# Decoder-layer kernel: key roots of the cached sequences on GpSimd as a power, page numbers read once

## The chip, the cores and the metric

The kernel runs on one core of one Trainium2 chip. The core has a TensorE (PE), which multiplies matrices out of SBUF into PSUM, a VectorE (DVE), a ScalarE (ACT), a GpSimd (POOL) and a SyncE (SP), whose queue here issues nearly all loads. Each engine works through its own instructions in order and waits on semaphores of the others. The metric is device microseconds of one execution.

## The reference, cut to what matters

One layer of a decoder is applied to 512 prompt positions and to 8 cached sequences of 4 new positions each (544 columns in all). The part at issue is the attention of the new positions over a paged latent cache of 2048 rows, 16 pages of 128 rows per sequence:

```python
def decompress(latent, lw):
    kv = (latent @ lw['w_kvb']).reshape(*latent.shape[:-1], H_A, NOPE_DIM + V_DIM)
    return rmsnorm(kv[..., :NOPE_DIM], lw['g_kn']), kv[..., NOPE_DIM:]

def one(args):                       # one cached sequence
    pt, qn, qr, lat_n, kr_n = args
    lat = jnp.concatenate([cache_latent[layer, pt].reshape(past, KV_LORA), lat_n], 0)
    kr = jnp.concatenate([cache_krope[layer, pt].reshape(past, ROPE_DIM), kr_n], 0)
    k_nope, v = decompress(lat, lw)
    s = (jnp.einsum('qhd,khd->hqk', qn, k_nope) + jnp.einsum('qhr,kr->hqk', qr, kr)) * scale
    ...
    p, _ = softmax_stats(s)
    return jnp.einsum('hqk,khd->qhd', p, v)
```

`rmsnorm` of a key of 64 numbers divides it by the root of its mean square plus 1e-6. Every cached key of every one of the 8 heads needs such an inverse root: 2048 rows x 8 heads per sequence.

## The kernel before

**The program as a whole.** Input projections, query projection, norms and rotations come first (to about 341 us), then the attention of the prompt (341 to 493 us), the eight cached sequences (493 to about 801 us), and then the output projection, the feed-forward part and the last gate (to the end). The matmuls of the projections are made of three products of split numbers (`mm3`, L494).

**A cached sequence (b = 0..7).** The keys themselves are not normed. The scores are taken by absorbed queries straight from the transposed latent page (`pgT`), and then multiplied by the inverse root of each key, so the keys are made only for the sum of their squares. For each of 16 pages t:

- ACT rounds the page to its upper half (`page_hi`, L737), DVE makes the lower half (`page_lo`, L1272), three pages ahead;
- PE makes the page's 512 raw key numbers in 6 matmuls (`page_keys`, L999), into one of two halves of `ps[0]`;
- ACT squares them (`page_square`, L744) into one of two halves of `sqK`, and DVE adds them up to 8 columns of `ssq` (`page_sums`, L1278).

PE may begin page g only when page g-2 is squared, and ACT may square page g only when page g-2 is summed.

**Behind the 16 pages.** PE takes the scores (`scores`, L1015, L1019) and the window scores (`win_scores`, L1031). ACT takes the root of the 128 x 128 numbers of `ssq` (`key_root`, L748). DVE, in its `scores` (L1283 and on), waits for that root, takes the reciprocal (L1284), transposes it to the layout of the scores (L1285), multiplies the scores by it (L1289) and finds row maxima, up to `mX` (L1300).

**The tails.** The rest of sequence b is laid between the pages of sequence b+1: PE at page 2 takes `row_max` (L1040, needs `mX`), at page 7 `values` (L1050 needs the exponentials and the window values `cV`; L1056 the latent pages `pgL`), at page 11 `turned` (L1065, L1068). ACT at page 3 takes the exponentials (L753, L754), at page 8 the scaled outputs. DVE at page 2 reads the maxima, at page 4 transposes the exponentials (L1311).

**The loads.** SP issues for each sequence, in this order: wait for the scores of the sequence before; pages 8 to 15 of this sequence (`load_pages`, L552); the window keys `cK` (L559); pages 0 to 7 of the next; wait for the values of the sequence before; 16 latent pages `pgL` (`load_latent`, L556); the window values `cV` (L562, L565). Each load of a page needs its page number, which SP reads from `ptab` into a register (`page_number`, L547): a TENSOR_LOAD and two instructions more. Each page is loaded twice, once as `pgT` and once as `pgL`, so its number is read twice.

**GpSimd.** It multiplies for the rotations (L421), issues the copies of the caches to the outputs (L614, L618) at marks of the other engines' progress, and has nothing to do between 461 and 898 us.

**The new rows.** The same inverse root is taken once for the 32 new rows (`rkN`): sums by DVE (L1194), root by ACT (L709), reciprocal by DVE (L1196), just ahead of the prompt's attention. DVE needs it in `p_new` (L1258) only, but the wait stands ahead of the loop.

Of the kernel before, what the change touches and what calls it, by code (L numbers as in the profile page):

```python
# [29 lines left out]
ACT = mybir.ActivationFunctionType  # L30
ALU = mybir.AluOpType
# [3 lines left out]
P = 128  # L35
D = 1024
KD = D // P
NP_ = 512
NB, NQ = 8, 4
NS = NB * NQ  # L40
T = NP_ + NS
HT = T // 2
H = 8
# [9 lines left out]
POOL = 160  # L53
# [16 lines left out]
RING = 24  # L70
NBUF = 4
AHEAD = 3
S_NEW, S_WIN, S_WNEW, S_ALL = 512, 544, 768, 800


# [30 lines left out]
def build(nc, x, cst, gains, win, wqb, wk, wv, wkt, wo, wgu, wdn, wdn2, wpl, plt, pgt, pgl, ck, cv, pt,  # L106
          y, o_lat, o_kr, o_ks, o_vs, o_ck, o_cv):
    with ExitStack() as ctx:
# [12 lines left out]
        def sb(name, shape, dt=F32):  # L121
            n = 1
            for x in shape[1:]:
                n *= x
            return at(name, shape, room(n), dt)

        def sem(name):
            return ctx.enter_context(nc.semaphore(name))
# [59 lines left out]
        mr, m2, nm, den, rec = (sb(n, [P, 2]) for n in ("rowmax", "rowmax2", "negmax", "den", "recip"))  # L188
        mX = sb("mX", [P, 2, 4])
        warm = sb("warm", [P, 1])  # L190
        st = sb("st", [P, 16])
        ptab = sb("ptab", [1, NB * NPG], I32)

# [26 lines left out]
        p_qg, p_ab, p_all = (sem(n) for n in ("prep_qg", "prep_absorb_mm", "prep_all"))  # L220
        q_ab, p_new, p_nw, z_new, k_raw, k_sq, k_ss, k_rt = (sem(n) for n in (
            "queries_laid", "new_scores_mm", "new_scores", "new_rows_cleared", "kraw_mm", "kraw_sq", "kraw_ssq", "key_root"))
        m_sc, w_sc, m_sub, w_max, m_x, m_mx, m_nm, m_e, m_et = (sem(n) for n in (
            "mla_scores", "win_scores", "mla_scores_read", "win_scores_read", "rowmax_masked", "max_mm", "max_read",
            "exp", "exp_turned"))
# [301 lines left out]
        @block.sync  # L527
        def _(sp):
            sp.dma_start(hT[:, 0:2, :], x[:, 0:2, :]).then_inc(s_x[0], 16)
            sp.dma_start(G[:, :], gains).then_inc(s_g, 16)  # L530
            sp.dma_start(C[:, 0:C_MA], cst[:, 0:C_MA]).then_inc(s_c, 16)
            for k in range(1, KD // 2):
                sp.dma_start(hT[:, 2 * k:2 * k + 2, :], x[:, 2 * k:2 * k + 2, :]).then_inc(s_x[k], 16)
            for u in range(2):
                sp_weight(W_IN + u, win[u])
            sp.dma_start(C[:, C_MA:], cst[:, C_MA:]).then_inc(s_c2, 16)
            sp.dma_start(wK[:, :, :], wk).then_inc(s_wk, 16)
            sp.dma_start(wV[:, :, :], wv).then_inc(s_wk, 16)
            sp.dma_start(ptab[:, :], pt).then_inc(s_pt, 16)
            for u in range(2, NIN):  # L540
                sp_weight(W_IN + u, win[u])
            for u in range(H):
                sp_weight(W_QB + u, wqb[u])
            for u in range(2):
                sp_weight(W_O + u, wo[u])
            def page_number(b, t):
                return bass.ds(sp.value_load(ptab[0:1, b * NPG + t:b * NPG + t + 1], min_val=0, max_val=POOL - 1), 1)  # L547

            def load_pages(b, ts):
                for t in ts:  # L550
                    s = (b * NPG + t) % RING
                    sp.dma_start(pgT[:, s, :], pgt[page_number(b, t), :, :].rearrange("a p n -> p (a n)")).then_inc(pg_in[s], 16)  # L552

            def load_latent(b):
                for t in range(NPG):
                    sp.dma_start(pgL[:, t, :], pgl[page_number(b, t), :, :].rearrange("a p n -> p (a n)")).then_inc(pl_in, 16)  # L556

            def load_win_k(b):
                sp.dma_start(cK, ck[b, :, :, PAST - W_TAIL:PAST].rearrange("c p n -> p c n")).then_inc(ck_in, 16)  # L559

            def load_win_v(b):
                sp.dma_start(cV[:, 3:NTW, :], cv[b, PAST - REC:PAST, :].rearrange("(j p) n -> p j n", p=P)).then_inc(cv_in, 16)  # L562
                for u in range(3):
                    old = cv[b, u * P * 4:(u + 1) * P * 4, :].rearrange("(g r) n -> g r n", r=16)
                    sp.dma_start(cV[:, u, :], old[:, 0:4, :]).then_inc(cv_in, 16)  # L565

            sp.wait_ge(s_pt, 16)
            sp.wait_ge(cq_lo, KQ)
            load_pages(0, range(11))
            sp.wait_ge(a_pv, 4 * H)  # L570
            sp.dma_start(wkT, wkt).then_inc(s_wkt, 16)
            load_win_k(0)
            sp.wait_ge(p_read, 2)
            load_latent(0)
            sp.wait_ge(a_o, H)
            sp.wait_ge(out_s, 80)
            sp.wait_ge(p_nw, 1)
            load_pages(0, range(11, NPG))
            load_pages(1, range(RING - NPG))
            load_win_v(0)  # L580
            for b in range(1, NB):
                sp.wait_ge(m_sc, b)
                load_pages(b, range(RING - NPG, NPG))
                sp.wait_ge(w_sc, b)
                load_win_k(b)
                if b + 1 < NB:
                    load_pages(b + 1, range(RING - NPG))
                sp.wait_ge(m_pv, b)
                load_latent(b)
                sp.wait_ge(w_pv, b)  # L590
                load_win_v(b)
            for u in range(2, KD):
                sp_weight(W_O + u, wo[u])
            sp.wait_ge(w_pv, NB)
            sp.dma_start(plT, plt).then_inc(s_plt, 16)
            sp_weight_loop(W_GU, 2 * HALVES[0], wgu[0:2 * HALVES[0]])
            sp_weight_loop(W_DN, KD, wdn)
            sp_weight_loop(W_GU2, 2 * HALVES[1], wgu[2 * HALVES[0]:])
            sp_weight_loop(W_DN2, KD, wdn2)
            sp_weight_loop(W_PL, KD, wpl)  # L600
            for m in range(KD):
                sp.wait_ge(pl_ev[m % 2], m // 2 + 1)
                sp.dma_start(y[m], hT[:, m, :]).then_inc(out_y, 16)
            sp.wait_ge(out_y, 16 * KD)

        @block.gpsimd
        def _(pool):
# [9 lines left out]
            def copy_v(b, z):  # L617
                pool.dma_start(o_cv[b, z * HALF:(z + 1) * HALF, :],  # L618
                               cv[b, NQ + z * HALF:NQ + (z + 1) * HALF, :]).then_inc(out_c, 16)

            pool.memset(vNew[:, :], 0.0).then_inc(z_new, 1)
            pool.memset(latNew[:, :], 0.0).then_inc(z_new, 1)
            pool.wait_ge(z_new, 2)
# [7 lines left out]
            for g in g_qh:  # L631
# [8 lines left out]
            pool.dma_start(o_cv[:, PAST - NQ:PAST, :].rearrange("b q n -> b (q n)"),  # L640
                           vNew[0:NS, :]).then_inc(out_s, 16)
            pool.wait_ge(out_s, 80)
            for k in range(8):
                pool.wait_ge(a_s, 8 * k + 1)
                copy_v(k // 2, k % 2)

            for b in range(4, NB):
                for k in range(4):
# [5 lines left out]
        def _(act):  # L654
# [50 lines left out]
            act.activation(tmp[0:NS, 0, 0:512], ps[0][0:NS, 0, :], ACT.Square).then_inc(kn_sq, 1)  # L705
            act.wait_ge(tn_mm, 1)
            act.activation(latNew[0:NS, :], ps[0][0:NS, 1, 0:KVL], ACT.Copy).then_inc(tn_ev, 1)
            act.wait_ge(kn_ss, 1)
            act.activation(rkN[:, :], rkN[:, :], ACT.Sqrt, scale=1.0 / NOPE, bias=G[0:NS, G_EPS:G_EPS + 1]).then_inc(k_rt, 1)  # L709


            for n in range(len(units) + 4):
# [30 lines left out]
                    act.wait_ge(k_ss, g - 1)  # L743
                act.activation(sqK[:, g % 2, :], ps[0][:, g % 2, :], ACT.Square).then_inc(k_sq, 1)  # L744

            def key_root(b):
                act.wait_ge(k_ss, (b + 1) * NPG)
                act.activation(ssq[:, b % 2, :], ssq[:, b % 2, :], ACT.Sqrt, scale=1.0 / NOPE,  # L748
                               bias=G[:, G_EPS:G_EPS + 1]).then_inc(k_rt, 1)

            def exps(b):
                act.wait_ge(m_nm, b + 1)
                act.activation(E[:, 0:S_WIN], S[:, 0:S_WIN], ACT.Exp, bias=nm[:, 0:1], accum_out=den[:, 0:1])  # L753
# [12 lines left out]
            for b in range(NB):  # L766
                for t in range(NPG):
                    page_square(b, t)
                    if b * NPG + t + AHEAD < NB * NPG:
                        page_hi(*divmod(b * NPG + t + AHEAD, NPG))  # L770
                    if b and t in act_tail:
                        act_tail[t](b - 1)
                key_root(b)
            for t in act_tail:
                act_tail[t](NB - 1)
            sqrt_table()
# [369 lines left out]
        def _(v):  # L1146
# [46 lines left out]
            v.wait_ge(kn_sq, 1)  # L1193
            v.tensor_reduce(rkN[:, :], tmp[0:NS, 0, 0:512].rearrange("p (h d) -> p h d", h=H), AX.X, ALU.add).then_inc(kn_ss, 1)  # L1194
            v.wait_ge(k_rt, 1)
            link(v.reciprocal(rkN[:, :], rkN[:, :]))  # L1196
            for n in range(len(units) + 5):
                if n >= 2 and n - 2 < len(units):
                    m = n - 2
# [33 lines left out]
                    link(v.memset(qwS, 0.0))  # L1233
                if n == 20:
                    v.wait_ge(n_rope, ropes_before[-1])
                    v.tensor_scalar(qg[:, :, :], QT[LOW, :, NP_:T], G[LOW, G_K:G_K + 1], None, ALU.mult).then_inc(p_read, 1)
                    for j in range(4):
                        last = v.tensor_copy(qrB[32 * j:32 * j + 32, :, 32 * j:32 * j + 32].rearrange("p b (h q) -> p h b q", h=H),
                                             QT[MID, :, NP_:T].rearrange("p h (b q) -> p h b q", q=NQ))
                    last.then_inc(p_read, 1)  # L1240
                    v.wait_ge(p_read, 2)
                    v.sem_inc(q_ab, 1)
# [37 lines left out]

            def scores(b):

                v.wait_ge(k_rt, b + 2)  # L1283
                link(v.reciprocal(ssq[:, b % 2, :], ssq[:, b % 2, :]))  # L1284
                link(v.transpose(RK, ssq[:, b % 2, :].unsqueeze(2).broadcast_to([P, NPG * H, NQ])))  # L1285
                v.wait_ge(m_sc, b + 1)
                if b:
# [277 lines left out]
```

## Time and profile before

| | us |
|---|---|
| median of 3 runs | 1374.35 |
| lowest, highest | 1372.84, 1376.12 |
| the profiled execution | 1373.12 |
| its span, first to last instruction | 1371.3 |
| PE busy in it | 1263.7 |
| DVE busy | 593.0 |
| ACT busy | 485.9 |
| POOL busy | 45.7 |
| mean granted TensorE clock | 0.926 of 2.4 GHz |

All times in the rows are from the start of the span of that one execution. A busy time of PE is modelled from the starts of its matmuls, so PE shows busy also where it paces nothing; who waits for whom tells more. Only the stretch from 493 to 801 us holds the work that is changed, together with a few instructions at 342 us.

### The profile page before, as it was taken

To read this page: it belongs to the slowest core of one execution; us is meant where nothing else is said; L and a number is where in the kernel's file an instruction comes from. 1 tells how busy PE (TensorE), PEld (TensorE's weight loads), DVE (VectorE), ACT (ScalarE), POOL (GpSimd) and SP (SyncE) were. 2 spreads that over 40 slices of the span, in tenths; PEclk is the share of its full clock that TensorE was granted. 3 is DMA by queue.
4 is the path that set the end of the run, shared out by engine and by line. 5 is a ranking of instruction groups with operands and counts; after the bars stand their busy time and mean duration, and the time that the engine had idled before them with its cause. 6 is when DMAs were issued, how large, how long until landed. Compare 5 with 4: busy or idle time off the path is not lost.

```text
span 1371.3 us, 22076 instructions
## 1 busy us (share of the span) xinstructions
PE 1263.7 (92%) x8308; PEld 1034.4 (75%) x8308; DVE 593.0 (43%) x1095; ACT 485.9 (35%) x861; POOL 45.7 (3%) x60
## 2 busy tenths in 40 slices
PE   5999989999999999998889778799999999999798
PEld 4988976434655576665566458699999999999788
DVE  4223221644774456665556435643332223333543
ACT  4223243101653355554455332333332112222332
POOL 0000000321000000000000000000000000000000
PEclk8999999956997589999999968899999999999899
DMA  6773312002445135666566602155464354562122
GB/s 236 251 271 141 116 36 87 0 1 83 184 164 213 61 110 159 224 225 204 181 216 198 223 26 70 66 201 201 165 208 175 138 180 157 199 225 97 57 77 85
DMA packets 68820, 202.70 MB, mean 148 GB/s; under 512 B 7457, under 2 KB 40226, under 8 KB 67394
## 3 DMA queue, kind: packets, MB, share of 16 engines
q1 hardware_dynamic: 66562, 131.74, 28.9%
q0 software_dynamic: 2176, 69.90, 14.1%
q8 instruction: 48, 0.79, 0.2%
q14 instruction: 34, 0.28, 0.1%
HBM read 196.53 MB, written 72.13 MB: 196 GB/s over the span
## 4 chain that ended last, share of the span: by engine, by line
PE 72%; SPq 14%; DVE 6%; issue 5%; ACT 1%; DMA 1%; DVEq 0%; ACTq 0%
PE ps L494 48%; SPq L547 7%; PE ps L947 4%; PE ps L387 4%; PE ps L967 4%; SPq L556 3%; SPq L552 3%; PE ps L398 3%; PE ps L956 2%; PE ps L410 2%; PE ps L999 2%; DVE R L435 1%; DVE tmp L452 1%; DVE aLo L353 1%; PE ps L911 1%
## 5 line engine op out<-in xcount | busy, mean ns | idle before, releaser
L494 PE MATMUL ps<-aHi,wHi 128*128 128x272 f32 (+1 forms) x1392 | 296.7, 295 | 37.2 <-DVE aLo L353 33.8
L494 PE MATMUL ps<-aHi,wLo 128*128 128x272 f32 (+1 forms) x1392 | 292.7, 292 | 0.0
L494 PE MATMUL ps<-aLo,wHi 128*128 128x272 f32 (+1 forms) x1392 | 291.7, 291 | 0.0
L494 PEld LDWEIGHTS ps<-aHi,wHi 128*128 128x128 f32 (+1 forms) x1392 | 220.7, 190 | 47.2 <-issue 19.5
L366 DVE TENSOR_TENSOR wLo<-ring,wHi 128x1024 fp32r<-128x1024 f32 (+3 forms) x105 | 133.4, 1271 | 211.5 <-ACT wHi L361 211.5
L494 PEld LDWEIGHTS ps<-aLo,wHi 128*128 128x128 f32 (+1 forms) x1392 | 222.0, 190 | 0.0
L494 PEld LDWEIGHTS ps<-aHi,wLo 128*128 128x128 f32 (+1 forms) x1392 | 220.6, 191 | 0.0
L361 ACT ACTIVATE wHi<-ring 128x1024 fp32r<-128x1024 f32 (+3 forms) x105 | 114.5, 1091 | 196.3 <-PE ps L494 196.2
L1278 DVE TENSOR_REDUCE ssq<-att 128x8 f32<-128x512 f32 x128 | 87.4, 683 | 97.2 <-ACT att L744 96.1
L744 ACT ACTIVATE att<-ps 128x512 f32<-128x512 f32 x128 | 76.3, 596 | 117.7 <-PE ps L999 117.1
L999 PE MATMUL ps<-wkHi,pgHi 128*128 128x512 f32 x256 | 103.2, 403 | 11.6 <-ACT att L744 10.4
L999 PE MATMUL ps<-wkHi,pgLo 128*128 128x512 f32 x256 | 100.0, 391 | 0.0
L999 PE MATMUL ps<-wkLo,pgHi 128*128 128x512 f32 x256 | 99.7, 390 | 0.0
L494 PE MATMUL ps<-hidHi,wLo 128*128 128x272 f32 x352 | 72.9, 288 | 0.0
L494 PE MATMUL ps<-hidHi,wHi 128*128 128x272 f32 x352 | 72.7, 288 | 0.0
L387 PE MATMUL ps<-sq,C 128*128 128x272 f32 (+5 forms) x196 | 59.7, 458 | 14.2 <-ACT sq L295 14.2
L494 PE MATMUL ps<-hidLo,wHi 128*128 128x272 f32 x352 | 72.6, 288 | 0.0
L999 PEld LDWEIGHTS ps<-wkHi,pgHi 128*128 128x128 f32 x256 | 48.1, 188 | 25.9 <-issue 15.7
L724 ACT ACTIVATE att<-att,st 128x128 f32<-128x128 f32 (+1 forms) x64 | 36.0, 562 | 67.5 <-DVE st L1217 66.6
L1362 DVE TENSOR_TENSOR sq<-ps,tmp 128x544 f32<-128x544 f32 x22 | 16.0, 725 | 101.3 <-ACT tmp L803 101.3
L737 ACT ACTIVATE pgHi<-big 128x256 fp32r<-128x256 f32 x128 | 52.3, 410 | 19.2 <-DMA big<-in_pgt 19.2
L1272 DVE TENSOR_TENSOR pgLo<-big,pgHi 128x256 fp32r<-128x256 f32 x128 | 53.0, 416 | 13.8 <-ACT pgHi L737 13.8
(181 smaller groups left out, 1521.5 us busy)
## 6 DMA issues: line engine op xcount, KB each, us to landing
out_o_cv<-in_cv POOLq DMA_DIRECT2D x16, 2044.0 KB, 8.3
ring<-in_wgu SPq DMA_DIRECT2D x44, 512.0 KB, 3.5
big<-in_pgt SPq DMA_DIRECT2D x128, 144.0 KB, 2.8
big<-in_pgl SPq DMA_DIRECT2D x128, 128.0 KB, 2.0
kv<-in_ck SPq DMA_DIRECT2D x8, 1792.0 KB, 8.5
ring<-in_win SPq DMA_DIRECT2D x21, 512.0 KB, 4.2
kv<-in_cv SPq DMA_DIRECT2D x8, 1024.0 KB, 5.5
kv<-in_cv SPq DMA_DIRECT2D x24, 256.0 KB, 5.7
```

Of the source, the lines that this page charges most:

```text
L361: nc.scalar.activation(wHi[:, u % 2, 0:width], ring[:, u % 2, 0:width], ACT.Copy).then_inc(w_hi, 1)
L366: nc.vector.tensor_tensor(wLo[:, u % 2, 0:width], ring[:, u % 2, 0:width], wHi[:, u % 2, 0:width].bitcast(F32), ALU.subtract).then_inc(w_l ...
L387: last = nc.tensor.matmul(ps[2][out, a, 0:hw], ones, sq[rows, k % 2, a * hw:(a + 1) * hw], start=(j == 0 and t == 0), stop=(j == len(q["sr ...
L494: ins = nc.tensor.matmul(pair[rows, a, 0:HT], w[:, c], xx[:, k, a * HT:(a + 1) * HT], start=(k == 0 and z == 0), stop=(k == nk - 1 and z = ...
L547: return bass.ds(sp.value_load(ptab[0:1, b * NPG + t:b * NPG + t + 1], min_val=0, max_val=POOL - 1), 1)
L737: act.activation(pgHi[:, g % NBUF, :], pgT[:, g % RING, 0:KVL], ACT.Copy).then_inc(p_hi, 1)
L744: act.activation(sqK[:, g % 2, :], ps[0][:, g % 2, :], ACT.Square).then_inc(k_sq, 1)
L947: mm(ps[0][:, n % 2, 0:(i + 1) * P], q[:, i * P:(i + 1) * P], k[:, 0:(i + 1) * P], start=True, stop=True).then_inc(a_s, 1)
L967: last = mm(ps[2][r, (h // 2) % 2, i * P:(i + 1) * P], v[:, j, (h % H) * HD:(h % H + 1) * HD], prT[:, m % 2, j * P:(j + 1) * P], start=(j ...
L999: last = mm(ps[0][:, g % 2, :], x_[:, g % NBUF, c * P:(c + 1) * P], w_[:, c, :], start=(c == 0 and z == 0), stop=(c == KC - 1 and z == 2))
L1272: v.tensor_tensor(pgLo[:, g % NBUF, :], pgT[:, g % RING, 0:KVL], pgHi[:, g % NBUF, :].bitcast(F32), ALU.subtract).then_inc(p_lo, 1)
L1278: v.tensor_reduce(ssq[:, b % 2, t * H:(t + 1) * H], sqK[:, g % 2, :].rearrange("p (h d) -> p h d", h=H), AX.X, ALU.add).then_inc(k_ss, 1)
```

## The change

- The page number is kept in a register from its first reading for `pgT` until its reading for `pgL`, and not read again. The eleven numbers of sequence 0 that are read first, and every later pair, follow this; five of sequence 0 are read twice, since their latent pages are asked for first.
- ACT's `key_root` is gone and with it DVE's reciprocal of `ssq`. GpSimd adds 64 x 1e-6 to the sums and raises them to the power -1/2, first for the 12 pages that are summed first (128 x 96 numbers), then for the other 4 (128 x 32). DVE waits for the second one.
- The same for `rkN` (32 x 8), ahead of GpSimd's eight copies of the window values, behind its wait for the outputs of the states.
- The power is taken of the sum, not of the mean, so the absorbed queries are multiplied by 8 (the root of 64), in an instruction that was there.

```diff
+EARLY = 12
+        minus_half = sb("minus_half", [P, 1])
+        z_half, k_eps = sem("half_set"), sem("ssq_eps")
-            def page_number(b, t):
-                return bass.ds(sp.value_load(ptab[0:1, b * NPG + t:b * NPG + t + 1], min_val=0, max_val=POOL - 1), 1)
+            numbers = {}
+
+            def page_number(b, t, last=False):
+                if (b, t) not in numbers:
+                    numbers[b, t] = sp.value_load(ptab[0:1, b * NPG + t:b * NPG + t + 1], min_val=0, max_val=POOL - 1)
+                return bass.ds(numbers.pop((b, t)) if last else numbers[b, t], 1)
...
-                    sp.dma_start(pgL[:, t, :], pgl[page_number(b, t), :, :].rearrange("a p n -> p (a n)")).then_inc(pl_in, 16)
+                    sp.dma_start(pgL[:, t, :], pgl[page_number(b, t, True), :, :].rearrange("a p n -> p (a n)")).then_inc(pl_in, 16)
...
+            pool.memset(minus_half[:, :], -0.5).then_inc(z_half, 1)
...
             pool.wait_ge(out_s, 80)
+            def inverse_root(sums, rows, cols, n):
+
+                pool.tensor_scalar(sums, sums, NOPE * EPS, None, ALU.add).then_inc(k_eps, 1)
+                pool.wait_ge(k_eps, n)
+                pool.tensor_tensor(sums, sums, minus_half[rows, 0:1].broadcast_to([rows.stop, cols]), ALU.pow).then_inc(k_rt, 1)
+
+            pool.wait_ge(z_half, 1)
+            pool.wait_ge(kn_ss, 1)
+            inverse_root(rkN[:, :], slice(0, NS), H, 1)
             for k in range(8):
                 pool.wait_ge(a_s, 8 * k + 1)
                 copy_v(k // 2, k % 2)
+
+            for b in range(NB):
+                pool.wait_ge(k_ss, b * NPG + EARLY)
+                inverse_root(ssq[:, b % 2, 0:EARLY * H], FULL, EARLY * H, 2 * b + 2)
+                pool.wait_ge(k_ss, (b + 1) * NPG)
+                inverse_root(ssq[:, b % 2, EARLY * H:], FULL, P - EARLY * H, 2 * b + 3)
...
-            act.wait_ge(kn_ss, 1)
-            act.activation(rkN[:, :], rkN[:, :], ACT.Sqrt, scale=1.0 / NOPE, bias=G[0:NS, G_EPS:G_EPS + 1]).then_inc(k_rt, 1)
...
-            def key_root(b):
-                act.wait_ge(k_ss, (b + 1) * NPG)
-                act.activation(ssq[:, b % 2, :], ssq[:, b % 2, :], ACT.Sqrt, scale=1.0 / NOPE,
-                               bias=G[:, G_EPS:G_EPS + 1]).then_inc(k_rt, 1)
...
-                key_root(b)
...
             v.wait_ge(k_rt, 1)
-            link(v.reciprocal(rkN[:, :], rkN[:, :]))
...
-                    v.tensor_scalar(qg[:, :, :], QT[LOW, :, NP_:T], G[LOW, G_K:G_K + 1], None, ALU.mult).then_inc(p_read, 1)
+                    v.tensor_scalar(qg[:, :, :], QT[LOW, :, NP_:T], G[LOW, G_K:G_K + 1], NOPE ** 0.5, ALU.mult,
+                                    ALU.mult).then_inc(p_read, 1)
...
-                v.wait_ge(k_rt, b + 2)
-                link(v.reciprocal(ssq[:, b % 2, :], ssq[:, b % 2, :]))
+                v.wait_ge(k_rt, 2 * b + 3)
                 link(v.transpose(RK, ssq[:, b % 2, :].unsqueeze(2).broadcast_to([P, NPG * H, NQ])))
```

**SP, from the last page load `pgT` to the first latent pages `pgL`.** Before:

```order
L552 ISA
L552 DMA big<-in_pgt 128x288
L547 TENSOR_LOAD ptab
L547 ISA x2
L556 ISA
L556 DMA big<-in_pgl 128x256
```

In the change (the same place; L553 is the reading of a number, L559 `pgT`, L563 `pgL`):

```order
L553 TENSOR_LOAD ptab
L553 ISA x2
L559 ISA
L559 DMA big<-in_pgt 128x288
L563 ISA
L563 DMA big<-in_pgl 128x256
L563 ISA
L563 DMA big<-in_pgl 128x256
```

The three instructions that read the number are gone ahead of each latent page; those ahead of the `pgT` pages stay.

**ACT, from the last pages of a sequence to the exponentials of its tail.** Before (L748 is the root, L753 and L754 the exponentials, L744 a square, L737 a page's upper half):

```order
L737 ACTIVATE pgHi<-big 128x256
L748 ACT_TABLE_LOAD
L748 ACTIVATE ssq<-ssq,G 128x128
L744 ACTIVATE att<-ps 128x512
...
L753 ACT_TABLE_LOAD
L753 ACTIVATE C,den<-C,negmax 128x544
L754 ACTIVATE C,den<-C,negmax 128x256
L744 ACTIVATE att<-ps 128x512
```

In the change (L765 is a square, L758 an upper half, L769 and L770 the exponentials):

```order
L765 ACTIVATE att<-ps 128x512
L758 ACTIVATE pgHi<-big 128x256
L769 ACTIVATE C,den<-C,negmax 128x544
L770 ACTIVATE C,den<-C,negmax 128x256
L765 ACTIVATE att<-ps 128x512
```

The root is gone from ACT's order, and so are both table loads, here and at every sequence.

**GpSimd, in the stretch of the cached sequences, where it had nothing before.** In the change, two sequences:

```order
L653 TENSOR_SCALAR ssq<-ssq 128x96
L655 TENSOR_TENSOR ssq<-ssq,minus_half 128x96
L653 TENSOR_SCALAR ssq<-ssq 128x32
L655 TENSOR_TENSOR ssq<-ssq,minus_half 128x32
L653 TENSOR_SCALAR ssq<-ssq 128x96
```

The additions and powers stand between the eight copies of window values and the copies of the feed-forward stretch.

## Rows read from the trace of the kernel before

**Rows 1.** Waits of PE, 519 to 800 us: us in total, times, longest.

```profile
PE ps L1050 <- DMA kv<-in_cv: 19.3, 5, 5.2
PE ps L999 <- ACT att L744: 10.4, 7, 1.5
PE ps L1040 <- DVE mX L1300: 1.9, 1, 1.9
```

**Rows 2.** Waits of SP's queue, whole span: the longest of the stage.

```profile
SPq L547 <- PE ps L1019: 8.7, 1, 8.7
```

**Rows 3.** Windows from scores to scores: us, busy PE, PEld, DVE, ACT, POOL, clock, DMA.

```profile
550.30:585.00 34.70, 32.95 (x231) 23.79 (x230) 21.25 (x49) 19.36 (x41) 0.00 (x0) 1.00 0.67 222
...
619.80:660.60 40.80, 35.88 (x235) 24.75 (x235) 21.49 (x50) 19.36 (x41) 0.00 (x0) 0.92 0.63 204
660.60:699.40 38.80, 34.62 (x235) 24.20 (x238) 21.51 (x50) 19.35 (x41) 0.00 (x0) 0.96 0.66 211
699.40:737.30 37.90, 32.94 (x235) 24.08 (x235) 21.47 (x50) 19.36 (x41) 0.00 (x0) 1.00 0.66 210
737.30:777.90 40.60, 34.60 (x235) 24.18 (x235) 21.15 (x48) 18.75 (x39) 0.00 (x0) 0.96 0.61 199
```

**Rows 4.** Timeline of SP's issues: start, us, what; one round's pages and latent pages, and five rounds later.

```profile
557.87 7.96 SPq L552 DMA_DIRECT2D big<-in_pgt  x8
...
576.12 16.69 SPq L556 DMA_DIRECT2D big<-in_pgl  x16
...
752.84 8.53 SPq L552 DMA_DIRECT2D big<-in_pgt  x8
```

**Rows 5.** SP's instructions for a page number and a latent page: ns min/median/max.

```profile
L547 SPq TENSOR_LOAD <-ptab x256: 262/268/472, 217.5 to 780.6; - x128
L547 SPq FUSED_REGOPS  x256: 152/152/187, 218.0 to 781.2; - x128
...
L556 SPq DMA_DIRECT2D big<-in_pgl x128: 328/333/3114, 407.0 to 781.6; - x128
```

**Rows 6.** Timeline of ACT about the exponentials of one tail.

```profile
596.56 1.28 ACT L753 ACT_TABLE_LOAD   x1
...
599.09 0.57 ACT L744 ACTIVATE att<-ps 128x512 f32<-128x512 f32 x1
```

**Rows 7.** Timeline of DVE from a sequence's last sums to its `mX`; row_max on PEld.

```profile
584.42 0.69 DVE L1278 TENSOR_REDUCE ssq<-att 128x8 f32<-128x512 f32 x1 [0.34 <-ACT att L744]
...
585.78 0.69 DVE L1278 TENSOR_REDUCE ssq<-att 128x8 f32<-128x512 f32 x1 [0.34 <-ACT att L744]
...
587.80 0.95 DVE L1284 RECIPROCAL ssq<-ssq 128x128 f32<-128x128 f32 x1 [1.00 <-ACT ssq L748]
588.78 0.71 DVE L1285 STREAM_TRANSPOSE C<-ssq 128x512 f32<-128x512 f32 x1
...
591.66 0.17 DVE L1300 TENSOR_TENSOR mX<-C,rowmax 128x8 f32<-128x8 f32 x1
...
592.25 0.42 PEld L1040 LDWEIGHTS ps<-mX,C 128*128 128x128 f32 x2
```

**Rows 8.** Timeline of the tail of the last sequence, PE and DVE.

```profile
786.39 1.01 DVE L1311 STREAM_TRANSPOSE big<-C 128x800 f32<-128x800 f32 x1 [1.40 <-ACT C L754]
...
790.00 2.78 PE L1050 MATMUL ps<-kv,big 128*32 128x512 f32 x11 [5.21 <-DMA kv<-in_cv]
```

**Rows 9.** Timeline of POOL: its first, a usual and its longest multiplication.

```profile
144.04 2.33 POOL L421 TENSOR_TENSOR tmp<-big,C 32x544 f32<-32x544 f32 x1 [8.54 <-DVE big L459]
238.66 1.34 POOL L421 TENSOR_TENSOR tmp<-big,C 128x544 f32<-128x544 f32 x1 [92.28 <-DVE big L459]
...
271.88 3.37 POOL L421 TENSOR_TENSOR tmp<-big,C 128x544 f32<-128x544 f32 x1 [2.75 <-DVE big L476]
```

**Rows 10.** Timeline at the new rows' root, DVE and ACT.

```profile
342.61 0.19 DVE L1196 RECIPROCAL rkN<-rkN 32x8 f32<-32x8 f32 x1 [0.37 <-ACT rkN L709]
...
342.60 1.28 ACT L724 ACT_TABLE_LOAD   x1
```

## The prediction

> **What bounds the kernel now.** I first asked where PE waits while the cached sequences run, since its matmuls fill most of the span. Between 519 and 800 us the waits [rows 1] name two causes that matter: 19.3 us in five waits on the window values `cV`, and 10.4 us in seven waits of at most 1.5 us on ACT's squares. The first is not a slow transfer. SP's own waits [rows 2] show that it stood still for 8.7 us once, at the start of the stage, and nowhere else in it for over 2 us: SP issues all the time, and what it issues last in a round comes late. Its round is (752.84 - 557.87) / 5 = 38.99 us [rows 4]. The windows from scores to scores [rows 3] show the other limit. The second sequence takes 34.7 us at full clock with no wait on a load, as do the first and the third (515.5 to 619.8 us for the three, 34.75 each). There SP still lives on its lead. From the fourth on they take 40.8, 38.8, 37.9 and 40.6 us, and the clock falls in three of them. So the bound is **PE at 34.75 us a sequence while SP is ahead, and SP at 39 when its lead is used up**.
>
> **The page numbers.** A latent page takes SP (16.69 - 0.33) / 15 = 1.09 us, of which the issue itself is 0.333 [rows 4, 5]. The reading of a number is 0.268 + 0.152 us of instructions and the short gaps between them: at least 0.42, at most 1.09 - 0.33 = 0.76 us. I take 0.57, which leaves 0.15 for a check of the number and the gaps. Sixteen times this, 9.1 us, leaves a round: 38.99 - 9.1 = 29.9 us (26.8 to 32.3 by the two bounds). All of these are under PE's 34.75, so SP has to wait again and is no bound by any of the bounds. Behind a reading stand only SP's own loads. With SP ahead, the four late sequences take 34.75 us like the first three: 158.1 - 139.0 = **19.1 us less**. Of this 14.1 us are four of the waits on `cV` [rows 1, 3]; the rest is the halved clock that came with them. What comes late next? The loads have room: latent pages every 0.52 us are 252 GB/s while they last, which is above the 222 GB/s of a round of 34.7 us, but the DMA engines were busy for 0.67 of that round [rows 3], and nobody waits for a latent page within 20 us of its issue.
>
> **The table loads.** Without a root on ACT the order has no table load in the sequences. The one at the root costs nothing on the path: ACT waits for PE behind it. The other stands ahead of the exponentials: 1.28 us, and the square behind it starts at 599.09 [rows 6]. PE waits at most 1.5 us for that square, seven times, 10.4 us together [rows 1]. The two exponentials themselves stay. So 7 x 1.28 = **9.0 us less** (10.4 at most, if the whole wait goes), and a sequence becomes 34.75 - 1.28 = 33.47 us, still above SP's 29.9. The eighth load, at the last tail, was hidden. In the row the exponential follows its load without idle time. The Trainium skill (ScalarE: Activation LUTs, What ACT_TABLE_LOAD costs) gives 1283 ns for the load, as here, and 1380 ns of drain beside it for every switch; with a drain on the path the saving would reach the cap of 10.4 us, and the trace has no room for it.
>
> **The root moved to GpSimd.** From the end of a sequence's last sums (585.78 + 0.69 = 586.47) to the start of the transposition (588.78) pass 2.31 us: the rest of the table load, the root, and a reciprocal of 0.95 us [rows 7]. `mX` is ready at 591.83, and PE loads it at 592.25 without waiting. So the new path may take 2.31 + 0.42 = 2.73 us before PE waits. It holds an addition and a power of 128x32, if the power of 128x96, begun four pages earlier, is done. A page is 585.78 - 584.42 = 1.36 us, four are 5.44. No row shows a power on GpSimd. The nearest are its multiplications [rows 9]: 1.34 us for 544 columns, 2.5 ns a column, and 3.37 us, 6.2 ns a column, at its slowest. By either, both parts are over in under 0.8 us, and DVE goes on about 1.9 us earlier than before, which PE does not feel, since it did not wait. A power is surely more work than a product, so these rows are poor bounds above. What decides is the break-even: the first part is hidden up to 5.44 / 96 = 56 ns a column, the second up to some (2.73 - 0.2) / 32 = 79 ns; together PE waits from about 61 ns, **24 times a multiplication**. I take it below that, and the cost as 0. DVE also loses eight reciprocals, which lie in the same path. What GpSimd has queued behind these waits are its copies of the feed-forward stretch, at 898 us.
>
> **The last tail.** After the last sequence nothing covers these steps. PE waited 1.9 us for `mX` [rows 1]; I let it come 1.0 us earlier (0 at 61 ns a column, 1.9 at the price of the multiplication). The transposed exponentials were ready at 786.39 + 1.01 = 787.40, the matmuls started at 790.00 for want of `cV` [rows 8]: 2.6 us. **3.6 us less.** The clock was at half in much of 785 to 833 us; if it falls less, up to 3 us more are won, which I only put in the range.
>
> **The new rows.** DVE waited 0.37 us for ACT, and took 0.19 for the reciprocal [rows 10]. GpSimd now does two instructions of 8 columns in its place. Its wait for the state outputs stands ahead, but it issued its next copy at 343 us only since PE's first scores came then. The table load for the first exponential, 1.28 us from 342.60, no longer has to follow the root and may come earlier. Between -0.5 and +1.0 us (the first multiplication took 2.33 against 1.34 [rows 9]); I take 0. The rescaled queries cost the same instruction.
>
> **The sum.** 19.1 + 9.0 + 3.6 = 31.7 us. The profiled execution took 1373.12 us, 1.2 below the median of the runs; 1373.1 - 31.7 = 1341.4, and against the median **1342.6**.
>
> **Rivals.**
> First, **the power is slow**. This is the way to a slower kernel. With c ns a column, the path is 0.4 + 128c - 5.44 us once the first part is late, and its excess over 2.73 us falls on PE eight times, since `row_max` stands in PE's order ahead of page 2. At 75 ns it is 1.8 us, 15 in all: 1357. At 91 ns (37 multiplications) the 31.7 us are used up. Beyond that the kernel is slower; at 123 ns (50 multiplications) 8.0 x 8 = 64 us against 31.7: 1406. [...]
> Second, **the change does not do what it says for SP**: the issues take back what the readings gave up. One issue of a latent page took 3.11 us [rows 5], at a time when a copy between caches ran. If the round stays at 39 us, PE stays bound by SP, the table loads are hidden too, and the time is 1370 to 1374. Against it: in the stage sixteen issues took 16.69 us without one that blocked.
> Third, **ACT's wait does not go**, since the two exponentials or DVE's transposition end it anyway: 9 us less gain, 1351.
> Fourth, **the first power is slow once**. The row shows 1.0 us more for GpSimd's first multiplication: 1343.6. The Trainium skill (GPSIMD Engine Reference, 2.1 Instruction dispatch) gives about 6 us for the first call of freshly loaded code; by it, ahead of the prompt's attention and uncovered, the time would be near 1348.
>
> **How the numbers follow.** Forecast 0.64; slow power with part of the gain left 0.10, with none 0.08; SP's round unchanged 0.05; ACT's wait stays 0.06; a slow first power, by several us, 0.07. The range reaches up over the third and fourth rival and to 75 ns a column, and down by the clock and the upper bounds of the savings (1.4 + 0.9 + 0.5 + 3, and a little for a steadier clock in the sequences): 1335 to 1358. A measurement of this kernel can tell about 0.2%, 2.7 us, from no change. Faster by more: 0.64 + 0.10 + 0.06 + 0.07 and half of SP's case, 0.89. Within: 0.03. Slower: 0.08.
>
> **What would show it.** SP waits again for scores or values in every round, some 3 us in each. Scores follow scores every 33.5 us in all eight sequences, at full clock, and no wait on `cV` is left, also in the tail. PE's seven waits on the square shrink to about 0.2 us. GpSimd's power of 128x96 takes under 5.4 us and that of 128x32 under 2.5. PE never waits for `mX` in the sequences. Wrong would be the forecast if PE waits at `row_max`, if the latent pages still come 1.09 us apart, or if a load named in PE's waits has taken SP's place.

## The result

The change makes the kernel slower: 1475.1 us (median of 4 runs, 1471.7 to 1477.3) against 1374.9 before, a ratio of 1.073 (95% interval 1.070 to 1.075). The forecast was 1342.6 us, with a range up to 1358. What came is the first rival, far out: the power on GpSimd costs 160 ns a column, 65 times a multiplication. The two savings in the sum are real, as the experiments below show, and near it in total, though one came out 4 us smaller than forecast and the other 3 us larger: with both of them and the roots left on ScalarE, the kernel takes 1343.8 us.

The changed kernel's page, its first part and one group of the fifth (name, shape, count | busy us, mean ns):

```profile
span 1475.4 us, 21708 instructions
PE 1279.9 (87%) x8308; PEld 1045.9 (71%) x8308; DVE 583.1 (40%) x1086; ACT 461.1 (31%) x836; POOL 223.2 (15%) x95
...
L655 POOL TENSOR_TENSOR ssq<-ssq,minus_half 128x96 f32<-128x96 f32 (+1 forms) x16 | 168.7, 10547 | 1.3
```

POOL is busy for 223.2 us, where it had 45.7. It is busy for 15% of the span and still sets the pace, which only the waits show. Those of PE, 519 to 910 us (us in total, times, longest):

```profile
PE ps L1055 <- DVE mX L1314: 113.2, 8, 16.7
PE ps L1065 <- DVE big L1325: 4.5, 8, 2.7
```

The 19.3 us on `cV` and the 10.4 us on ACT's squares of [rows 1] are gone, both of them. In their place PE waits 113.2 us for `mX`, eight times. And `mX` is late because DVE, which works in order, has to stop ahead of the transposition until GpSimd is done. The timelines of POOL and DVE about the end of the second sequence, which answer to [rows 7]:

```profile
568.34 0.56 POOL L653 TENSOR_SCALAR ssq<-ssq 128x96 f32<-128x96 f32 x1 [26.65 <-DVE ssq L1293]
568.99 15.66 POOL L655 TENSOR_TENSOR ssq<-ssq,minus_half 128x96 f32<-128x96 f32 x1
584.73 0.29 POOL L653 TENSOR_SCALAR ssq<-ssq 128x32 f32<-128x32 f32 x1
585.10 5.43 POOL L655 TENSOR_TENSOR ssq<-ssq,minus_half 128x32 f32<-128x32 f32 x1
...
573.03 0.69 DVE L1293 TENSOR_REDUCE ssq<-att 128x8 f32<-128x512 f32 x1 [0.34 <-ACT att L765]
...
590.57 0.71 DVE L1299 STREAM_TRANSPOSE C<-ssq 128x512 f32<-128x512 f32 x1 [16.52 <-POOL ssq L655]
593.44 0.17 DVE L1314 TENSOR_TENSOR mX<-C,rowmax 128x8 f32<-128x8 f32 x1
```

The last sums end at 573.72. The first part of the power, begun when 12 pages were summed, ends only at 584.65, 10.9 us behind them, and the second runs after that. From the last sums to the transposition pass 16.85 us, where it was 2.31 and could be 2.73.

The windows from scores to scores (columns as in [rows 3]) show the sequences. They alternate between 48.9 and 50.0 us, and the clock is down:

```profile
523.40:572.30 48.90, 34.76 (x233) 24.89 (x232) 20.18 (x49) 16.27 (x38) 22.00 (x5) 0.86 0.50 148
572.30:622.30 50.00, 35.92 (x235) 25.74 (x237) 20.20 (x49) 16.26 (x38) 21.98 (x5) 0.83 0.54 170
622.30:671.20 48.90, 34.80 (x231) 24.92 (x230) 20.10 (x48) 16.27 (x38) 21.88 (x5) 0.86 0.53 167
```

Where the 104.1 us of the span come from, by the starts of the same matmuls in both traces: 7.9 by the first scores (523.4 against 515.5; 3.2 of these are there already when PE begins the prompt's scores, at 345.07 against 341.86, ahead of every changed instruction of this stage, 1.6 are the root of the new rows; beside the rest stands a longer stretch at half clock, 27.3 us from 336.4 on, where it was 17.1 us from 331.4 on), 83.4 in the seven sequences that follow (345.7 against 262.3), 12.5 in the last tail, up to the matmuls that turn the summed latents into outputs (36.1 against 23.6). What comes after is the same within 0.3.

### The profile page after: what moved, and what is told of

Read it like the earlier page. It is cut to its first block, busy times and chain, and to the rows that moved or that the text cites. A ratio compares the mean times of both kernels' runs of the same rounds, so it can differ in the third digit from the quotient of the medians.

```text
span 1475.4 us, 21708 instructions
## 1 busy us (share of the span) xinstructions
PE 1279.9 (87%) x8308; PEld 1045.9 (71%) x8308; DVE 583.1 (40%) x1086; ACT 461.1 (31%) x836; POOL 223.2 (15%) x95
## 4 chain that ended last, share of the span: by engine, by line
PE 75%; POOL 12%; DVE 9%; ACT 2%; issue 1%; DMA 0%; SPq 0%; DVEq 0%; ACTq 0%; POOLq 0%
PE ps L497 45%; POOL ssq L655 11%; PE ps L1014 7%; PE ps L390 4%; PE ps L962 4%; PE ps L982 3%; PE ps L401 2%; PE ps L971 2%; PE ps L413 2%; DVE R L438 1%; PE ps L1071 1%; DVE tmp L455 1%; PE ps L1065 1%; PE ps L926 1%; DVE aLo L356 1%
## 5 line engine op out<-in xcount | busy, mean ns | idle before, releaser
L497 PE MATMUL ps<-aHi,wHi 128*128 128x272 f32 (+1 forms) x1392 | 296.5, 295 | 38.1 <-DVE aLo L356 34.7
L655 POOL TENSOR_TENSOR ssq<-ssq,minus_half 128x96 f32<-128x96 f32 (+1 forms) x16 | 168.7, 10547 | 1.3
L765 ACT ACTIVATE att<-ps 128x512 f32<-128x512 f32 x128 | 76.4, 597 | 242.4 <-PE ps L1014 241.9
L1014 PE MATMUL ps<-wkHi,pgHi 128*128 128x512 f32 x256 | 108.9, 426 | 1.6 <-DVE pgLo L1287 1.2
L1014 PE MATMUL ps<-wkLo,pgHi 128*128 128x512 f32 x256 | 104.7, 409 | 0.0
L1014 PE MATMUL ps<-wkHi,pgLo 128*128 128x512 f32 x256 | 104.5, 408 | 0.0
L1055 PE MATMUL ps<-mX,C 128*128 128x8 f32 x16 | 4.8, 372 | 113.2 <-DVE mX L1314 113.2
L1055 PEld LDWEIGHTS ps<-mX,C 128*128 128x128 f32 x16 | 4.0, 311 | 116.6 <-DVE mX L1314 116.6
L621 POOL DMA_DIRECT2D out_o_ck<-in_ck x16 | 8.1, 507 | 419.4 <-PE ps L497 419.4
L1014 PEld LDWEIGHTS ps<-wkHi,pgHi 128*128 128x128 f32 x256 | 51.9, 203 | 17.1 <-issue 5.6
```

The costliest lines, as they stand in the source:

```text
L497: ins = nc.tensor.matmul(pair[rows, a, 0:HT], w[:, c], xx[:, k, a * HT:(a + 1) * HT], start=(k == 0 and z == 0), stop=(k == nk - 1 and z = ...
L655: pool.tensor_tensor(sums, sums, minus_half[rows, 0:1].broadcast_to([rows.stop, cols]), ALU.pow).then_inc(k_rt, 1)
L1014: last = mm(ps[0][:, g % 2, :], x_[:, g % NBUF, c * P:(c + 1) * P], w_[:, c, :], start=(c == 0 and z == 0), stop=(c == KC - 1 and z == 2))
```

## The experiments

Each is timed beside the kernel before on the same chip: 1374.3 us for the first four, 1376.3 for the last two.

### The page numbers read once, alone

The kernel before with this edit:

```diff
+            numbers = {}
+
+            def page_number(b, t, last=False):
+                if (b, t) not in numbers:
+                    numbers[b, t] = sp.value_load(...)
+                return bass.ds(numbers.pop((b, t)) if last else numbers[b, t], 1)
...
-                    sp.dma_start(pgL[:, t, :], pgl[page_number(b, t), :, :]...
+                    sp.dma_start(pgL[:, t, :], pgl[page_number(b, t, True), :, :]...
```

> The kernel before with the page numbers read once, and nothing else: the roots stay on ScalarE. My theory of the kernel before (SyncE is the bound from the fourth cached sequence on): the four late sequences fall from 158.1 to 139.0 us, and the last tail no longer waits for the window values, 2.6 us. 1374.9 - 21.7 = 1353 us, scores follow scores every 34.75 us, and no wait on the window values is left. Rival (the issues take back what the readings gave up): latent pages still about 1.09 us apart, 1372 to 1375 us.

Measured: 1356.1 us, ratio 0.987 (0.985 to 0.989). The saving is 18 us of the 21.7 expected. All seven sequences take 34.7 us at full clock. Two of the windows, two of SP's issues of 16 latent pages, and two of its waits:

```profile
590.70:625.40 34.70, 32.94 (x231) 23.82 (x230) 21.29 (x50) 19.33 (x41) 0.00 (x0) 1.00 0.74 238
729.60:764.30 34.70, 32.94 (x235) 23.83 (x237) 20.95 (x48) 18.73 (x39) 0.00 (x0) 1.00 0.67 212
...
542.76 8.05 SPq L560 DMA_DIRECT2D big<-in_pgl  x16
...
681.21 9.13 SPq L560 DMA_DIRECT2D big<-in_pgl  x16
...
SPq L550 <- PE ps L1023: 36.8, 7, 8.4
SPq L560 <- PE ps L1060: 8.5, 1, 8.5
```

SP, which waited 8.7 us once [rows 2], now waits for the scores in each of the seven rounds, 36.8 us together. The rival is out: the latent pages are (8.05 - 0.33) / 15 = 0.51 to 0.59 us apart (the prediction had 0.52), where they were 1.09.

### The table of the exponentials loaded early, roots left on ScalarE

```diff
+        def exp_table():
+            nc.scalar.activation(warm[:, :], G[:, G_EPS:G_EPS + 1], ACT.Exp)
...
                 key_root(b)
+                exp_table()
```

> The kernel before with the page numbers read once, and, behind ScalarE's root of each sequence, one exponential of a 128x1 tile that nobody reads, so that the table of the exponentials is loaded there, where ScalarE has 3.5 us to spare, and not ahead of the real exponentials. Roots stay on ScalarE, reciprocals on VectorE. Theory (the saving of the changed kernel's ScalarE part was real and is to be had without GpSimd): seven times 1.28 us less than with the numbers alone, 1353 - 9 = 1344 us, scores follow scores every 33.5 us. Rival (the two exponentials end the wait anyway): the same 1353 us as with the numbers alone.

Measured: 1343.8 us, ratio 0.977 (0.974 to 0.979), 12 us below the numbers alone. Timeline of ACT at the end of the third sequence, and at the exponentials:

```profile
587.13 1.28 ACT L756 ACT_TABLE_LOAD   x1
588.42 0.40 ACT L756 ACTIVATE ssq<-ssq,G 128x128 f32<-128x128 f32 x1
588.84 1.28 ACT L342 ACT_TABLE_LOAD   x1
590.13 0.20 ACT L342 ACTIVATE warm<-G 128x1 f32<-128x1 f32 x1
592.37 0.60 ACT L752 ACTIVATE att<-ps 128x512 f32<-128x512 f32 x1 [2.03 <-PE ps L1008]
...
597.49 0.74 ACT L761 ACTIVATE C<-C,negmax 128x544 f32<-128x544 f32 x1
```

Both loads now lie where ACT would be idle, and 2.0 us are still left there. The exponentials at 597.49 come without one ahead. The windows say what that is worth, and that nothing else took its place:

```profile
519.50:552.80 33.30, 32.96 (x232) 23.80 (x231) 21.30 (x50) 19.45 (x42) 0.00 (x0) 1.00 0.67 205
552.80:586.10 33.30, 32.96 (x232) 23.80 (x231) 21.30 (x50) 19.45 (x42) 0.00 (x0) 1.00 0.75 241
719.30:752.60 33.30, 32.96 (x232) 23.80 (x231) 20.96 (x48) 18.84 (x40) 0.00 (x0) 1.00 0.72 232
```

33.3 us each, of which PE is busy for 32.96. The prediction had 33.47 by taking off the 1.28 us of the load alone. The whole wait of 1.49 went, and the window became 1.4 us shorter, so the upper value of that term was nearer. This is the fastest version that was run.

### The power in seven parts

```diff
-EARLY = 12
+PARTS = (4, 2, 2, 2, 2, 2, 2)
...
+                done = 0
+                for i, n in enumerate(PARTS):
+                    pool.wait_ge(k_ss, b * NPG + done + n)
+                    inverse_root(ssq[:, b % 2, done * H:(done + n) * H], FULL, n * H, len(PARTS) * b + i + 2)
+                    done += n
...
-                v.wait_ge(k_rt, 2 * b + 3)
+                v.wait_ge(k_rt, len(PARTS) * (b + 1) + 1)
```

> The changed kernel with the powers in seven parts, of 4, 2, 2, 2, 2, 2 and 2 pages, in place of 12 and 4. Theory (only the price of the power, 160 ns a column and 0.32 us each as the profile of the changed kernel has it, and where it stands, make the loss): laid on the ends of the sums in the kernel before, the last part ends 4.45 us after the last sum where 12 and 4 pages end 16.9 after it; the excess over 2.73 us is 1.7 us a sequence, 14 us in all, and the new rows' root 1.6 us. 1343 + 16 = 1359 us. Rival (the power also disturbs the other engines, or the loss has another cause, in how GpSimd and VectorE share the memory): seven parts work longer beside VectorE than two and the kernel stays above 1400 us.

Measured: 1374.5 us, ratio 1.000 (0.998 to 1.002); 100 us faster than two parts, and 15 us slower than expected. The groups of POOL's powers, and three windows:

```profile
L655 POOL TENSOR_TENSOR ssq<-ssq,minus_half 128x16 f32<-128x16 f32 x48 | 140.1, 2919 | 4.0
L655 POOL TENSOR_TENSOR ssq<-ssq,minus_half 128x32 f32<-128x32 f32 x8 | 43.5, 5440 | 0.7
...
517.40:560.50 43.10, 35.68 (x231) 25.56 (x230) 20.12 (x48) 16.27 (x38) 30.20 (x19) 0.88 0.57 178
560.50:595.80 35.30, 33.33 (x235) 23.76 (x235) 20.23 (x49) 16.27 (x38) 25.16 (x15) 1.00 0.71 229
595.80:632.60 36.80, 34.81 (x235) 24.88 (x234) 20.16 (x49) 16.28 (x38) 25.11 (x15) 0.95 0.70 224
```

GpSimd works longer than in the change (183.6 us of powers against 168.7), with about a fifth of the loss or less in all sequences but the first (35.2 and 36.8 us against 33.3 without the powers, where the change has 48.9 and 50.0). So its work does not disturb the others; where its last part ends is what costs. The miss of 15 us lies mostly in two places that my expectation left out. The first sequence's sums have no tails between them and come faster than GpSimd can follow, so DVE waits 9.8 us for its root, PE 7.1, and the window is 43.1 us long (8 us of the miss). In the next six PE waits 1.6 us for `mX`, where 1.7 had been worked out, but the clock fell behind three of them all the same (36.8 us against 35.2; 5 us more). No other division was run. An estimate from these rows: the columns of a page take GpSimd 1.28 us, to which the start of a power (0.32) and an addition (0.26) come, and PE makes a page in 1.36 us; so GpSimd falls behind over the last pages however they are divided, and some wait is left.

### The wait filled with matmuls

In the changed kernel, 24 and then 32 matmuls that nobody reads:

```diff
             def row_max(b):
+                for _ in range(FILL):
+                    mm(ps[2][:, 1, 256:512], cm(C_ID), C[:, 0:256], start=True, stop=True)
                 pe.wait_ge(m_x, b + 1)
```

> The changed kernel with 24 matmuls of 256 columns ahead of each row_max on TensorE, whose result nobody reads, so that TensorE works through about 10 of the 14 us in which it waits for the maxima. Theory (the loss beyond the wait comes from the clock, which falls to half after each wait): the wait is as long, the clock stays up in the sequences, a sequence falls from 49.4 us to about 47.7, and the time by 12 to 16 us, to about 1461 us. Rival (the clock is not worth anything here, since PE has slack): the same within 3 us, 1475 us.

Measured: 1473.0 us, ratio 1.071 (1.068 to 1.074): no gain. By the figures I had put down the theory lost. But its trace shows that the test was incomplete. The wait was not gone, 3.4 us of it were left in each sequence. The half-clocked stretches were shorter (3.4 and 6.8 us in turn, where they had been 13.7 and 17.1), but only their part inside the wait was gone. The windows over two such stretches, in the change and then in this run, show the same work of PE at half clock, 3.3 and 5.6 us:

```profile
534.40:548.10 13.70, 3.29 (x9) 2.71 (x10) 4.69 (x13) 0.00 (x0) 7.12 (x3) 0.50 0.73 242
582.20:599.20 17.00, 5.54 (x14) 4.48 (x15) 5.78 (x16) 0.90 (x2) 8.17 (x3) 0.50 0.62 204
...
548.40:551.80 3.40, 3.35 (x9) 2.77 (x10) 1.85 (x4) 0.00 (x0) 0.00 (x0) 0.50 0.22 67
596.20:603.00 6.80, 5.61 (x14) 4.55 (x15) 3.94 (x14) 0.90 (x2) 0.00 (x0) 0.50 0.33 92
```

So the sequences took 49.0 and 50.0 us as before. Hence the second run.

> The changed kernel with 32 matmuls that nobody reads ahead of each row_max, not 24, so that the 3.4 us of wait that were left with 24 are filled too (0.43 us each). With 24 the sequences still alternated between 48.9 and 50.0 us, and the stretches at half clock had only become shorter, and lay in the working part. Theory (what a sequence takes beyond 33.3 + 13.8 = 47.1 us is work at half clock, which follows any idle stretch of some us): with no wait left the clock stays full in the sequences, they take 47.1 to 47.5 us each, and the time falls by 12 to 18 us, to about 1460 us. Rival (the extra 1.8 to 2.9 us of a sequence have another cause): 48.9 and 50.0 us again, 1473 us or more.

Measured: 1456.0 us, ratio 1.059 (1.056 to 1.062), 19 us less than the change. Two windows:

```profile
565.20:612.60 47.40, 47.08 (x295) 35.88 (x294) 20.20 (x49) 16.26 (x38) 21.97 (x5) 1.00 0.56 177
612.60:660.00 47.40, 47.08 (x297) 35.88 (x296) 20.19 (x49) 16.26 (x38) 21.96 (x5) 1.00 0.54 175
```

The clock is full throughout, and all seven sequences take 47.4 us: 33.3 and the wait of 13.8, and 0.3. So of the 16.1 us by which a sequence of the change is longer than 33.3 on average, about 13.8 are the wait itself, and 1.8 or 2.9 are work at half clock behind it. The 19 us are not all of this kind. The two profiles differ by 22.9 us: 14.1 lie in the seven sequences and 3.2 behind the last scores, while 5.6 lie ahead of the first scores (517.85 against 523.40), where no filling matmul stands.

### The power without the page numbers

The change with `page_number` as before.

```diff
-                return bass.ds(numbers.pop((b, t)) if last else numbers[b, t], 1)
+                return bass.ds(sp.value_load(...), 1)
```

> The changed kernel with every page number read twice again, as before: only the roots' part of the change is left. Theory (in the changed kernel a sequence lasts 49 us for the power's sake, and SyncE's old round of 39 us hides in that): the same as the changed kernel, 1475 us within 4. Rival (what the two parts do adds up): the 18 us that reading once gained alone come on top, 1493 us.

Measured: 1474.9 us, ratio 1.072 (1.070 to 1.075), as the change. What reading once saves is worth nothing here: the sequences take 49.1 to 50.1 us without it too, and SP's old round of 39 us fits into that.

## Why the prediction was wrong

**The step that failed** is the one on the root moved to GpSimd: "I take it below that, and the cost as 0". "That" was 24 times a multiplication. I had the condition (PE waits from about 61 ns a column) and no row for the price, and took the nearest rows, 2.5 and 6.2 ns, as telling which side it is on. The change's rows give 0.32 us and 160 ns a column: (15.66 - 5.43) / 64 for the slope; the two other widths, 16 columns at 2.92 us and the new rows' 8 at 1.67, lie on the same line within 0.1 us. The row of the multiplication said nothing of the price of the power; why the power costs so much no run shows. With no row for it, the two sides of the break-even should have had nearly even chances, and the range should have reached the slow side.

**The rival's arithmetic was right in form.** Put 160 ns in its formula, 0.4 + 128c - 5.44, and the path is 15.4 us; measured, 16.85 from the last sums to the transposition. The rest is the start of each power (0.32 us, twice), the additions (0.56 and 0.29 us, where I had 0.2 for each) and the steps between. The excess over 2.73 is then 14.1, and PE waited 13.8. Eight times 13.8 is 110 us less 31.7 saved: from 1374.9 that is 1454; measured 1475.

**What it left out is the clock.** I had seen that the halved stretches came with the waits on `cV`, and counted them there as 5 us. In the rival I did not: waits of 14 us are followed by work at half clock, and filling them gave back 14 us in the sequences and 3 behind them. With the 1.6 us of the new rows, 1454 and 17 and 2 are 1473.

**What held.** SP as the bound from the fourth sequence on: read once, all sequences took 34.7 us and no wait on `cV` was left. Its yield was 18 us where 19.1 + 2.6 had been summed. The spans of the two traces differ by 17.6, though 23.7 were gained in the stage (first to last scores in 243.0 against 262.3 us, the tail 4.4 more); 5.7 were lost in the stretch ahead of it, where the first scores came later (521.3 against 515.5). The table loads: 9.0 summed, 12.4 measured as the difference of two kernels, 9.9 in seven sequences (7 x 1.41). The DMA engines had room, as predicted: at 33.3 us a sequence they are busy for 0.67 to 0.79. One reading was off at no cost: a sequence's last latent page is used 10.5 us after its issue (592.48 and 603.01), not 20. The new rows' root was taken as 0, within -0.5 and +1.0; it is +1.6, above the upper bound, and by its width, not for being the first power. The first power took 1.67 us at 345.98, on the line of the later ones, so the fourth rival is out. The Trainium skill (GPSIMD Engine Reference, 2.1 Instruction dispatch) gives about 6 us for the first call of freshly loaded code; no such time appears there, and whether the power counts as such code no run shows. The Trainium skill (ScalarE: Activation LUTs, What ACT_TABLE_LOAD costs) puts a drain of about 1.38 us beside each switch of tables; in the early-load kernel there is none: root, load and exponential follow each other at 588.42, 588.84 and 590.13. The last tail was forecast with `mX` 1.0 us earlier; with the slow power that could not come, and with the roots on ScalarE PE still waits its 1.9 us.

**Not settled.** Why the first scores come later than in the profile of before (515.5 us) in the single profile of every other kernel, 517.4 to 527.0 us. They do so with and without GpSimd's part, so beyond the 1.6 us of the new rows the powers are not the cause. It enters every difference of two single profiles.

## What to carry to other kernels

- An operation for which no row exists has no price, however many rows of its engine there are. Work out from which price on it decides, and if the answer turns on it, measure that price by itself first: one instruction at two widths would have told.
- A wait of TensorE, where it sets the pace, can cost more than its length, because work at half clock may follow it. Here 13.8 us of wait cost 15.6 to 16.7, so a price for a new wait needs a term for the clock, also in the rivals.
- An experiment that shortens a wait does not test what the wait brings with it. With 3.4 of 13.8 us left the cost of the clock was unchanged; only with none left did it go.
- To be rid of a table load that stands in the way, move it, before moving the work: one exponential that nobody reads, put where ScalarE idles, gave what GpSimd's root was meant to give (1343.8 us, where the forecast with it was 1342.6).

## What the runs showed of the hardware

- GpSimd's power costs 160 ns a column and some 0.32 us to start, on 128 partitions at 16, 32 and 96 columns; the one row on 32 partitions, with 8 columns, lies on the same line. Its multiplication costs 2.5 ns a column, its addition of a constant about 4 (0.56 us at 96 columns, 0.29 at 32).
- DVE's sums take 0.68 us on average beside a running power, as without one, and its lower halves of the pages 0.42 us in both cases: the powers did not slow this work of VectorE.
- At waits of TensorE of 1.6 to 4.5 us stood stretches of 3.4 to 6.8 us at half clock, at times beginning only when the work had begun again (in seven parts at 605.66, behind a wait of 1.6 us that ended at 605.01), and at times none (in the kernel before, a wait of 3.5 us that ended at 719.21). Matmuls that nobody reads, over the whole wait, kept them out of the sequences; with 3.4 us of each wait left, nothing was won.
